# One layer of a streaming encoder: the last turn of the expert loops written out

## The reference

```python
logits = x2 @ w_router + b_router
top_vals, top_idx = lax.top_k(logits, 4)
gates = softmax(top_vals)
for each expert e, for the tokens routed to it:
    h = x2[tok] @ w_gu[e] + b_gu[e]          # 1024 -> 2048
    g = minimum(h[:, :1024], 7.0);  u = clip(h[:, 1024:], -7.0, 7.0)
    y = (u + 1.0) * (g * sigmoid(1.702 * g))
    out[tok] += gate * (y @ w_down[e] + b_down[e])   # 1024 -> 1024
h = layer_norm(alpha * x2 + out, ln3_g, ln3_b)
layer_norm: (x - mean) * rsqrt(var + 1e-5) * g + b
```

## Time and profile before

| what | value |
|---|---|
| timed runs, median (lowest, highest) | 1186.82 us (1186.78, 1189.0) |
| the profiled execution | 1187.33 us |
| its span, first to last instruction | 1185.5 us |
| mean granted clock of TensorE | 0.963 |
| TensorE matmuls, share of the span | 90% |
| VectorE, ScalarE, GpSimd | 31%, 14%, 3% |
| transfers | 445.12 MB, mean 375 GB/s |

### The profile page before, as it was taken

The page is one execution under the profiler, slowest core; times in us unless marked ns, Lnnn a source line. Parts: engine busy times, 40 slices in busy tenths (PEclk is TensorE's granted clock), DMA queues, the critical chain, the costliest instruction groups (busy, mean ns, idle before and its releaser), DMA issues.

```text
span 1185.5 us, 20125 instructions
## 1 busy us (share of the span) xinstructions
PE 1066.1 (90%) x7910; PEld 460.6 (39%) x7911; DVE 364.8 (31%) x1196; ACT 165.5 (14%) x374; POOL 31.2 (3%) x26
## 2 busy tenths in 40 slices
PE   9999999999998769999976669999979969998974
PEld 8668548653333213333321113333323313333321
DVE  0816241255323113333311113333313313333314
ACT  1113200311111001111100001111101101111101
POOL 0520000000000000000000000000000000000000
PEclk9999999999999899999998889999989989999997
DMA  9973274668999999999999999999999999799995
GB/s 329 369 269 142 72 286 175 268 236 341 428 429 428 427 430 427 430 427 429 428 428 430 427 431 426 429 428 430 428 428 430 426 431 427 299 431 427 430 427 237
DMA packets 48032, 445.12 MB, mean 375 GB/s; under 512 B 5200, under 2 KB 6480, under 8 KB 22704
## 3 DMA queue, kind: packets, MB, share of 16 engines
q1 hardware_dynamic: 45264, 439.86, 89.0%
q10 hardware_dynamic: 2752, 5.04, 1.3%
HBM read 443.84 MB, written 1.05 MB: 375 GB/s over the span
## 4 chain that ended last, share of the span: by engine, by line
PE 66%; DMA 28%; SPq 2%; DVE 1%; another core or an unknown queue 1%; issue 1%; ACT 0%
PE bank L792 21%; DMA ring<-in_w_down 16%; DMA ring<-in_w_gu 11%; PE bank L828 11%; PE bank L486 8%; PE bank L747 6%; PE bank L501 6%; PE bank L734 3%; PE bank L674 2%; SPq L361 2%; PE bank L740 2%; PE bank L581 1%; PE bank L803 1%; DMA ring<-in_w_mq 1%; PE bank L808 1%
## 5 line engine op out<-in xcount | busy, mean ns | idle before, releaser
L792 PE MATMUL bank<-ring,wk 128*32 128x512 f32 x3264 | 394.3, 631 | 87.2 <-DMA ring<-in_w_gu 87.2
L792 PEld LDWEIGHTS bank<-ring,wk 128*32 128x32 f32 x3264 | 104.9, 113 | 347.3 <-issue 214.2
L828 PE MATMUL bank<-ring,wk 128*32 128x512 f32 x1632 | 205.3, 595 | 0.0
L1428 DVE TENSOR_SCALAR wk<-bank 128x256 f32<-128x256 f32 x51 | 21.7, 425 | 563.9 <-PE bank L792 563.8
L747 PE MATMUL bank<-wk 64*128 64x512 f32 x416 | 105.2, 624 | 0.7 <-ACT wk L1029 0.7
L486 PE MATMUL bank<-ring 128*128 128x256 f32 x448 | 98.0, 380 | 1.4 <-issue 0.8
L828 PEld LDWEIGHTS bank<-ring,wk 128*32 128x32 f32 x1632 | 65.6, 109 | 64.1 <-issue 30.5
L486 PEld LDWEIGHTS bank<-ring 128*128 128x128 f32 x448 | 84.6, 190 | 13.2 <-issue 1.9
L1021 ACT ACTIVATE wk<-wk 128x256 f32<-128x256 f32 x51 | 21.2, 416 | 477.8 <-DVE wk L1428 477.8
L501 PE MATMUL bank<-ring 128*128 128x512 f32 x160 | 69.3, 593 | 0.0
L747 PEld LDWEIGHTS bank<-wk 64*128 64x128 f32 x416 | 36.7, 191 | 74.7 <-issue 73.0
(11 more groups left out here) (276 smaller groups left out, 692.8 us busy)
## 6 DMA issues: line engine op xcount, KB each, us to landing
ring<-in_w_gu SPq DMA_DIRECT2D x128, 2048.0 KB, 32.6
ring<-in_w_down SPq DMA_DIRECT2D x64, 2048.0 KB, 38.4
ring<-in_w_in SPq DMA_DIRECT2D x4, 2048.0 KB, 24.8
ring<-in_w_ck SPq DMA_DIRECT2D x2, 2048.0 KB, 24.3
ring<-in_w_cv SPq DMA_DIRECT2D x2, 2048.0 KB, 14.7
ring<-in_w_out SPq DMA_DIRECT2D x2, 2048.0 KB, 14.5
ring<-in_w_cq SPq DMA_DIRECT2D x2, 2048.0 KB, 9.1
ring<-in_w_co SPq DMA_DIRECT2D x2, 2048.0 KB, 7.8
```

Source lines behind the costliest of these rows:

```text
L792: ins = mm(hidden(g), xg[:, kk, c, :], gate_and_up(w[:, kk, :], g), start=False, stop=2 * c + kk == KT - 1, skip_group_check=True)
L828: ins = mm(strip(7, 2 * d + b), actT[:, b, 2 * c + gg, :], wd[:, gg, b, 512 * d:512 * d + 512], start=c == 0 and gg == 0 and b == 1, stop= ...
```

## The change

- SyncE's and TensorE's loops over the turns end one turn earlier, and the last turn is written out behind them.
- In the last turn's second expert (`ending`), nine `keep_warm` matmuls (here into bank 5) stand ahead of each of the gate/up pieces 2, 3 and 4. They come before the wait for that piece.
- The last down piece is loaded as two transfers of 1 MB with a semaphore each (`half_landed`, and the slot's own). The transposes now come ahead of the wait; then four matmuls wait for the first half and four for the second.
- The last normalisation is shared. Rows 0 to 127: VectorE subtracts the mean and applies the gain (`weighted`); ScalarE makes a diagonal matrix with the inverse deviations (`rstd_diag`); TensorE puts the shifts into banks 6 and 7 by a matmul with the identity, runs 14 `keep_warm` matmuls, then adds diagonal x rows to these banks; ScalarE copies the banks to `normal_rows` in slot 6, which is stored. Rows 128 to 255 stay on VectorE, scaled in two halves of 512 columns.
- The Newton step is done once for both halves of the rows.
- SyncE waits for the two copies of rows 0 to 127 (`final_ready` at 2), stores them, then waits for rows 128 to 255 (`last_ready` at 2) and stores these.

The diff, cut to its core:

```diff
@@ SyncE
+            def load_last(e, s):
+                src = w_down[bass.ds(e, 1), 1].rearrange("o p n -> (o p) n")
+                sp.dma_start(slot_words(s)[:, 0:half], src[:, 0:half]).then_inc(half_landed, 16)
+                sp.dma_start(slot_words(s)[:, half:SLOT], src[:, half:SLOT]).then_inc(slot_landed[s], 16)
...
-            with sp.Fori(1, LOOPS) as it:
+            with sp.Fori(1, LOOPS - 1) as it:
                 load_later(it * UNROLL, UNROLL * EXP_CHUNKS)
+            load_later((LOOPS - 1) * UNROLL, UNROLL * EXP_CHUNKS, ending=True)
...
-            for t in range(TT):
-                sp.wait_ge(final_ready, t + 1)
-                sp.dma_start(out[t * P:(t + 1) * P, :], res[:, t, :]).then_inc(stored, 16)
+            sp.wait_ge(final_ready, 2)
+            sp.dma_start(out[0:P, :], normal_rows).then_inc(stored, 16)
+            sp.wait_ge(last_ready, 2)
+            sp.dma_start(out[P:2 * P, :], res[:, 1, :]).then_inc(stored, 16)
@@ TensorE
+            def keep_warm(n):
+                for _ in range(n):
+                    mm(psum[5][:, Q:2 * Q], ident, late_c[:, 0:Q], start=True, stop=True)
...
                 for c in range(4):
+                    if ending and c > 0:
+                        keep_warm(9)
                     w = chunk(c).rearrange("p (j n) -> p j n", j=2)
...
                 for c in range(2):
-                    wd = chunk(4 + c).rearrange("p (g b n) -> p g b n", g=2, b=2)
                     if c == 1:
                         pe.wait_ge(xrows_ready, j + 2)
                         transpose_gathered()
+                    if c == 1 and ending:
+                        pe.wait_ge(half_landed, 16)
+                        wd = slot_words(RING_ORDER[(u * EXP_CHUNKS + 5) % RING])
+                    else:
+                        wd = chunk(4 + c)
+                    wd = wd.rearrange("p (g b n) -> p g b n", g=2, b=2)
                     for gg in range(2):
+                        if c == 1 and gg == 1 and ending:
+                            chunk(5)
...
             scatter(end=True)
+            shifts = ln3p[:, D:2 * D]
+            pe.wait_ge(ln_landed[2], 16)
+            for i in range(2):
+                mm(psum[6 + i][:], ident, shifts[:, 512 * i:512 * i + 512], start=True, stop=False)
+            keep_warm(14)
+            pe.wait_ge(spread_ready, 1)
+            for i in range(2):
+                pe.wait_ge(weighted, i + 1)
+                mm(psum[6 + i][:], rstd_diag, res[:, 0, 512 * i:512 * i + 512], start=False, stop=True).then_inc(shifted, 1)
@@ ScalarE
             rstd(2 * TT, 1)
+            act_e.wait_ge(scale_ready, 1)
+            af(rstd_diag, ident, ACT.Copy, scale=lrs[:, 0:1]).then_inc(spread_ready, 1)
+            for i in range(2):
+                act_e.wait_ge(shifted, i + 1)
+                af(normal_rows[:, 512 * i:512 * i + 512], psum[6 + i][:], ACT.Copy).then_inc(final_ready, 1)
@@ VectorE
-            for t in range(TT):
-                dve.wait_ge(var_ready, 2 * TT + t + 1)
...
-                link(newton(lrs[:, t:t + 1], lag[:, t, 1:2], 1, nwt[:, 8 + t:9 + t]))
...
+            dve.wait_ge(var_ready, 2 * TT + TT)
+            for i in range(2):
+                centre(0, i).then_inc(weighted, 1)
+            dve.wait_ge(lnlog_ready, 2 * TT + TT)
+            newton(lrs, lag[:, :, 1], 2, nwt[:, 8:10]).then_inc(scale_ready, 1)
+            for i in range(2):
+                ins = centre(1, i)
+            link(ins)
+            dve.wait_ge(scale_ready, 1)
+            for i in range(2):
+                c = slice(512 * i, 512 * i + 512)
+                v.scalar_tensor_tensor(out=res[:, 1, c], in0=res[:, 1, c], scalar=lrs[:, 1:2], in1=ln3p[:, D + 512 * i:D + 512 * i + 512], op0=ALU.mult,
+                                       op1=ALU.add).then_inc(last_ready, 1)
```

More of the change, by code:

```diff
@@ L117, in layer_program @@
         ln3p = S6[:, 0:2 * D]
+        normal_rows, rstd_diag = S6[:, 2 * D:3 * D], S6[:, 3 * D:3 * D + P]
         aqT = qbuf[:, 0:1024].rearrange("p (m t) -> p m t", m=4)
@@ L272, in layer_program @@
         dve_step, act_step, pool_step = sem("dve_step"), sem("act_step"), sem("pool_step")
-        stored, final_ready = sem("stored"), sem("final_ready")
+        stored, final_ready, last_ready = sem("stored"), sem("final_ready"), sem("last_ready")
+        half_landed = sem("half_landed")
+        weighted, spread_ready, scale_ready, shifted = sem("weighted"), sem("spread_ready"), sem("scale_ready"), sem("shifted")
         def columns(w, c0, n):
@@ L383, in _, with load_later @@
                 load_chunk(e, c, n)
-            def load_later(e0, chunks):
+            def load_later(e0, chunks, ending=False):
                 before = [divmod(n + UNROLL * EXP_CHUNKS - RING, EXP_CHUNKS) for n in range(chunks)]
@@ L393, in load_later @@
                     sp.nop(nofuse=True)
-                    load_chunk(experts[n // EXP_CHUNKS], n % EXP_CHUNKS, n)
+                    if ending and n == chunks - 1:
+                        load_last(experts[-1], RING_ORDER[n % RING])
+                    else:
+                        load_chunk(experts[n // EXP_CHUNKS], n % EXP_CHUNKS, n)
             sp.wait_ge(tables_ready, 1)
-            with sp.Fori(1, LOOPS) as it:
+            with sp.Fori(1, LOOPS - 1) as it:
                 load_later(it * UNROLL, UNROLL * EXP_CHUNKS)
+            load_later((LOOPS - 1) * UNROLL, UNROLL * EXP_CHUNKS, ending=True)
             sp.wait_ge(chunk_used[0], sp.value_load(cum_i[0:1, N_EXP - UNROLL:N_EXP - UNROLL + 1], min_val=1, max_val=MAX_PASSES))
             sp.dma_start(ln3p, ln_p[2:3].to_broadcast([P, 2 * D])).then_inc(ln_landed[2], 16)
-            for t in range(TT):
-                sp.wait_ge(final_ready, t + 1)
-                sp.dma_start(out[t * P:(t + 1) * P, :], res[:, t, :]).then_inc(stored, 16)
+            sp.wait_ge(final_ready, 2)
+            sp.dma_start(out[0:P, :], normal_rows).then_inc(stored, 16)
+            sp.wait_ge(last_ready, 2)
+            sp.dma_start(out[P:2 * P, :], res[:, 1, :]).then_inc(stored, 16)
             sp.wait_ge(stored, 16 * TT)
@@ L762, in _, with expert_pass @@
             pe.reg_mov(passes, 0)
-            def expert_pass(it, u):
+            def keep_warm(n):
+                for _ in range(n):
+                    mm(psum[5][:, Q:2 * Q], ident, late_c[:, 0:Q], start=True, stop=True)
+            def expert_pass(it, u, ending=False):
                 j = pe.snap(passes, min_val=0, max_val=MAX_PASSES)
@@ L831, in expert_pass, with all_passes @@
                 pe.reg_add(passes, passes, 1)
-            def all_passes(it, u):
+            def all_passes(it, u, ending=False):
                 n_passes = pe.value_load(npass_i[0:1, bass.ds(it * UNROLL + u, 1)], min_val=1, max_val=SEQ // SLOTS)
                 with pe.Fori(0, n_passes):
-                    expert_pass(it, u)
-            with pe.Fori(0, LOOPS) as it:
+                    expert_pass(it, u, ending)
+            with pe.Fori(0, LOOPS - 1) as it:
                 for u in range(UNROLL):
@@ L841, in _ @@
                     all_passes(it, u)
-            for u in range(N_EXP % UNROLL):
-                all_passes(LOOPS, u)
+            for u in range(UNROLL):
+                all_passes(LOOPS - 1, u, ending=u == UNROLL - 1)
             total = pe.snap(passes, min_val=1, max_val=MAX_PASSES)
@@ L1455, in _, with centre @@
             dve.wait_ge(ln_landed[2], 16)
-            for t in range(TT):
-                dve.wait_ge(var_ready, 2 * TT + t + 1)
-                for i in range(2):
-                    c = slice(512 * i, 512 * i + 512)
-                    ins = v.scalar_tensor_tensor(out=res[:, t, c], in0=psum[2 * t + i][:], scalar=lag[:, t, 0:1], in1=ln3p[:, c], op0=ALU.subtract, op1=ALU.mult)
-                link(ins)
-                dve.wait_ge(lnlog_ready, 2 * TT + t + 1)
-                link(newton(lrs[:, t:t + 1], lag[:, t, 1:2], 1, nwt[:, 8 + t:9 + t]))
-                v.scalar_tensor_tensor(out=res[:, t, :], in0=res[:, t, :], scalar=lrs[:, t:t + 1], in1=ln3p[:, D:2 * D], op0=ALU.mult,
-                                       op1=ALU.add).then_inc(final_ready, 1)
+            def centre(t, i):
+                c = slice(512 * i, 512 * i + 512)
+                return v.scalar_tensor_tensor(out=res[:, t, c], in0=psum[2 * t + i][:], scalar=lag[:, t, 0:1], in1=ln3p[:, c], op0=ALU.subtract, op1=ALU.mult)
+            dve.wait_ge(var_ready, 2 * TT + TT)
[8 more added lines that the diff above has]
+            for i in range(2):
+                c = slice(512 * i, 512 * i + 512)
+                v.scalar_tensor_tensor(out=res[:, 1, c], in0=res[:, 1, c], scalar=lrs[:, 1:2], in1=ln3p[:, D + 512 * i:D + 512 * i + 512], op0=ALU.mult,
+                                       op1=ALU.add).then_inc(last_ready, 1)
 def tables():
```

1 line of the change is left out of this document (added).

## The result

| kernel | median of the timed runs | ratio to before |
|---|---|---|
| before | 1187.28 us (7 runs, 1186.78 to 1189.0) | |
| changed | 1192.27 us (7 runs, 1190.59 to 1193.06) | 1.0039 [1.0029, 1.0048] |

The account below looks back on a forecast made before the run. TensorE and the expert-weight transfers were taken to hold 94% of the chain of waits. Tail +2.40 us and last scatter -0.28 gave +2.1; +2.0 was taken on the 1186.82 median, so 1188.8 us, range 1185.0 to 1190.8.

Parts of the forecast that it names:

- third part: Last turn of SyncE's and TensorE's loops: writing it out was taken to cost nothing.
- second rival: Written-out last turn: fetching its code makes an engine wait, about 2.6 us if late, 1189.7 to 1191.4 us; chance 0.16.
- 1.68 us of slack: TensorE's wait ahead of the last expert's first gate/up piece; a code delay there was to count only above 1.68 us.
- gate/up pieces apart, three times: Last expert: with nine fillers between them, pieces start 1.75 + 3.91 = 5.66 us apart, where before it was 4.89.
- fourth piece's start to the last scatter: Last expert on TensorE: from 1160.84 to the scatter's start at 1171.13, which was 0.28 us earlier than before.
- last scatter to the second store landed: Tail: 16.04 us from the scatter's start to the second store's landing, against 13.64 before, so +2.40.
- the fillers don't fit: Between the last expert's gate/up pieces: nine fillers cost 3.91 us, the wait they stand in is 2.97.
- the halves of the last piece: Last down piece: loading it in halves was taken to be worth nothing, and to cost nothing, as TensorE comes last.
- the tail's fillers outlast the diagonal: Tail on TensorE: fourteen fillers take 6.08 us and last 2.7 us too long after the diagonal matrix is there.
- VectorE's rows wait in SyncE's order for ScalarE's: Tail: SyncE waits for the first rows before looking at the second; VectorE was to be done 3 us before ScalarE.
- the stores then queue: End of the tail: two stores issued 0.35 us apart, the second landing 1.23 us after the first.
- first rival: Fillers take half the time and fit their waits: -1.6 to -2.5 us, median 1184.3 to 1185.2; chance 0.12.

Follow-up runs that it names:

- experiment 5: The kernel before with only SyncE's last turn written out, TensorE in its loop: 1187.09 us, ratio 1.0001.
- experiment 6: The kernel before with only TensorE's last turn written out, SyncE in its loop: 1188.56 us, ratio 1.0012.
- experiment 8: The kernel before plus, in each of SyncE's 15 turns, a transfer of two separate 16 KB rows that computes nothing: 1193.95 us, ratio 1.0062.
- C: The changed kernel, with the whole change in it: 1192.27 us, ratio 1.0039 to the kernel before.
- experiment 14: The changed kernel with the last down piece loaded and waited for as a whole: 1191.53 us, ratio 1.0037 to before.
- experiment 3: The changed kernel with 7 fillers in the tail in place of 14: 1189.37 us, ratio 1.0015 to before.
- experiment 10: The changed kernel with 6 fillers between the gate/up pieces and 7 in the tail, in place of 9 and 14: 1186.96 us, ratio 1.0003 to before.
- B: The kernel before the change: 1187.28 us.
- experiment 2: The changed kernel without the 27 fillers between the gate/up pieces: 1189.86 us, ratio 1.0023 to before.
- experiment 11: The changed kernel with its two stores swapped, rows 128 to 255 first: 1191.31 us, ratio 1.0033 to before.
- experiment 13: The changed kernel with four more fillers ahead of the last expert's first gate/up piece: 1191.22 us, ratio 1.0033 to before.
- experiment 12: The kernel before, loops untouched, with early transposes, shared last normalisation, four stores and no tail fillers: 1185.48 us, ratio 0.9981.

## Why the prediction was wrong

**The step that failed** is the third part: "I take nothing for it". Writing the turn out costs 1.2 us (1.0010, and 1.0012 for TensorE's part alone; 1.2 to 1.35 in the profiles from that landing near 353 us on). The prediction had the fetch of code as its second rival, with 0.16, but as a stall of TensorE's, to be looked for as a gap that no wait explains. There is none. It is the landing of the last expert's first piece that comes 0.8 to 1.5 us later, and since TensorE waits for that piece anyway, all of it counts. That TensorE's code is the cause, experiments 5 and 6 show; that its packet holds up one of the engines that carry the weights is argued from the packet's 1.1 us and from experiment 8, not seen. The prediction had the figure in its own row: 1.7% of 16 engines in 5 us is 1.36 us of one engine. It read the share as small because it was averaged over 16. "1.68 us of slack" was slack of TensorE, not of the transfers.

**Terms that were mis-sized.** From the start of the first piece in the profile of C:

| term | forecast | measured | difference |
|---|---|---|---|
| gate/up pieces apart, three times | 5.66 | 5.94 | +0.84 |
| fourth piece's start to the last scatter | 1160.84 to 1171.13 = 10.29 | 1161.69 to 1172.08 = 10.39 | +0.1 |
| last scatter to the second store landed | 16.04 | 12.72 + 3.6 = 16.32 | +0.3 |

A filler costs what was read from the rows, 0.434 (28 records in the tail take 6.05 from start to start). What was missing is the change between the two shapes of weights: from a piece to the first filler it is 1.86 us, not 1.75, and from nine fillers to the next piece 4.08, not 3.91. So 0.28 each time, which a run of one shape doesn't show. The 6.98 us of the earlier trace rows did hold one such change, from the last of four pieces to the scatter, and the division by four spread it.

**What was right.** The prediction said that the fillers don't fit, that TensorE ends up behind its transfers by the fourth piece, that the halves of the last piece are then worth nothing (experiment 14), that the tail's fillers outlast the diagonal by about 3 us, that VectorE's rows wait in SyncE's order for ScalarE's, and that the stores then queue. These steps add up to what the profile shows in the tail (+2.6 against +2.4 forecast) and explain what experiments 3 and 10 gave back (2.6 to 2.9 and 4 to 5 us). The first rival, fillers at half the price, fell by the second row of the profile. With it fell, for fp32, the figure of the Trainium skill ("TensorE: Matmul & The Clock Gate", Back-to-back issue gap) as the prediction had used it, 109 ns a record of 256 columns: 28 records from 1175.82 to 1181.87 are 216 ns each. The Trainium skill ("DMA: Bandwidth & Descriptors", Rules for kernel authors) says of two transfers to separate halves of the partitions that they serialise, because both run over all 16 engines. The two stores here take all partitions each, so they are a neighbouring case; the trace agrees for them: the second took 3.6 us from issue to landing, where one alone takes 2.6.

**The sum of what is known.** 2.1 forecast + 0.84 + 0.1 + 0.3 for the terms, + 0.8 for the packet and -0.3 for smaller shifts of the stream gives the 3.8 of the first profile. The timed runs differ by 4.6 us in the ratio, with an interval of 3.4 to 5.7, and by 5.0 in the medians; the second set of C's runs gives 4.4 and 4.9. The 3.8 lie inside the interval, so the terms leave no remainder that is clear of the noise. From the landing near 353 us on C takes 836.31 and 836.56 us and experiment 14's kernel 836.30, against 832.49 in B.

What could add to it are executions in which the first piece runs at half clock: TensorE's wait ahead of it has grown from 1.68 to 2.75 us, and two of the profiles with that wait (experiments 2 and 11) have the piece at 3.5 us. In experiment 11 the fillers make everything behind it follow, and those 1.5 us count in full. Experiment 13 agrees with this but can't be told from noise; how often it happens in the timed executions of C stays open.

**The range.** Its upper end took in most of the second rival's price on top of the likeliest sum (+4.0, where the rival went to +4.6), but the median under it was 0.5 us low and the errors all pointed one way. A term set to nothing, in code that no row had shown, should have widened it.

## What to carry to other kernels

- A filler has a length. Compute it from a row of the same type and shape, add the change of shape on both sides, and compare with the wait less what stands in it; one too many and TensorE is what is waited for from there on. Where the engine then waits for transfers or for another engine's result anyway, a half clock may cost nothing at all (experiment 12), so try none first.
- Code that is run once has to be fetched for that once. Here, where a saturated stream sets the pace, writing out TensorE's last turn delayed the stream; the loop, once loaded, costs nothing (in B no instruction packet lies between 315 us and the end). A share averaged over 16 engines hides a delay on one: multiply it by 16 and by the length of the window.
- When two engines share a last step, store in the order in which they finish, and in pieces.

## What the runs showed of the hardware

- One 16 KB packet of instructions takes 1.1 us of one DMA engine's time (3.4% of 16 engines in 2 us) beside a stream at 429 GB/s. Behind the first such packet of the written-out turn a piece lands 0.8 to 1.5 us later (eleven profiles); behind the second, at 1148 to 1149 us in B with TensorE's turn written out, the spacing stays at 4.89, and in experiment 10 it is 5.11 once. Two rows of 16 KB, in a transfer of only two rows, delay the stream by 0.48 us; one row of 16 KB makes 32 packets and delays it by 0.02 us (791.13 against 790.85 over the same stretch).
- Executions differ by up to 4.5 us before the last turn, also those of one kernel (4.05): the stream's landing near 353 us lay between 352.03 and 356.54 over the profiles. The two latest, 356.54 and 356.39, have a granted clock of 0.62 and 0.81 from 262 to 280 us and the others 0.91 or more; that the clock makes the difference is not shown. Comparing profiles from the first common landing takes this out.
- A wait of 2.97 us ahead of a piece doesn't by itself bring the half clock: in B the pieces behind such waits take 3.52 and 3.40 us, in experiment 5's profile the first piece behind one takes 1.92 (1149.34) and the next 3.41 (1154.24).
